# Halved weight units, squares moved behind the splits, and first loads on two queues in a streaming encoder step

## The chip, the cores and the metric

The kernel runs on one core of a Trainium2 chip. The metric is device time in microseconds (us), from runs without a profiler: the median of three runs of the kernel before is 1717.9 us (1715.5 to 1718.19). The engines are named PE (TensorE), DVE (VectorE), ACT (ScalarE), POOL (GpSimd) and SP (SyncE). Each works through its own list of instructions in order and meets the others only at semaphores.

## The reference, cut to what matters

One step of a two-layer encoder for 2048 prompt frames and 64 sample frames, 1024 features each, in float32. Layer A is a recurrent block, layer B attention over a short window.

```python
def _layer_a(x, ...):
    u = _rmsnorm(x, norm_g) @ w_in            # 1024 -> 2048
    xb, gate = jnp.split(u, 2, axis=-1)
    xc, new_buf = _causal_conv(xb, conv_buf, cw, cb)
    h, h_last = _rglru(xc, h0, ...)
    y = (h * silu(gate)) @ w_out
    return x + y, ...
# then k, v from one projection, and layer B: norm, projection to queries
# and gate, attention, output projection, residual
```

The change works on the first projection, `_rmsnorm(x, norm_g) @ w_in`, and on how all weights are prepared. The norm's factor of a frame is taken behind the matmul: the sum of squares over the features is made beside it, and the projection's result is multiplied by one over the root.

## The kernel before, in words

**Precision.** Every float32 matmul is made of three: a value is split into a high part (a copy in the matmul's rounded format, made by ACT) and a low part (the value less its high part), and high times high, low times high and high times low are summed. This holds for inputs and weights.

**Weights.** There are 54 units of 128 x 1024: unit u is one block of 128 output columns of a projection. Of these, 0 to 15 are the first projection's, 16 to 19 the gates', 20 and 21 the keys' and values', 22 to 29 the first output projection's, 30 to 45 the second projection's, 46 to 53 the last one's. A unit is loaded into `raw`, a buffer for two units (`load_unit`, a DMA issued by POOL); ACT makes the high part (`high_part`), and for units 0 to 3 DVE, for the others POOL, makes the low part (`low_part`); `low_units` is POOL's loop: low part of unit u, then the load of unit u+2, which waits until the low part of unit u is done. `VECTOR_UNITS` (4) is the number of units whose low part DVE makes. `w_high` and `w_split` count the finished parts, and PE waits for `w_split` before it uses a unit.

**The first projection.** The 2112 frames are worked in 6 tiles of 352. In step s the inputs of tile s are split while PE multiplies tile s-1. For each of a tile's 8 blocks of 128 features ACT makes the high part and then the square (`high_input`), DVE makes the low part and then adds the square to a running sum `acc` (`low_input`). There is one buffer `m.sq` for the square, so the square of block n waits until that of block n-1 has been added. Step 0 only splits: blocks 0 to 7, and behind blocks 0, 2, 4 and 6 the weight units 0 to 3, unit 4 behind block 7. In step 1, place j (0 to 15) PE multiplies unit j, ACT makes the high part of unit 5+j, and of input block j-3 of the next tile. After unit 0 PE sums `acc` over the features with a matmul by ones (L591), ACT takes the root (L410), DVE the reciprocal (L496). Only then does DVE start on the results: for j below 8 `branch` multiplies by the factor (L527) and makes the convolution (L531 to L561), for j from 8 it multiplies only (L514) and ACT applies SiLU (L433). PE has four result banks: unit j waits until result j-4 has been read.

**Later stages that the weights touch.** The last step of the projection (s = 6) splits units 16 to 26, the recurrent stage units 27 to 29 in turns of its own and 30 to 38 at its end, the second projection 39 to 45 and 46 to 53. In the recurrent stage POOL also makes parts of the scan's operands (L1031, L1039, L1042, L1050), in order with its weight work.

**Start of the program.** SP issues the loads of `vec`, `sink` and `halo` and then the 8 input blocks of tile 0; POOL issues units 0 and 1. ACT and DVE wait for all three small loads (`const_loaded`) before their first work on them.

## Time and profile before

| | |
|---|---|
| median of 3 runs | 1717.9 us |
| profiled execution, first to last instruction (span) | 1712.8 us |
| what lies around the span, by the median | 5.1 us |
| PE busy | 1612.5 us, 94% |
| PE weight load busy | 1457.1 us, 85% |
| DVE busy | 1182.5 us, 69% |
| ACT busy | 709.7 us, 41% |
| POOL busy | 393.2 us, 23% |

The profiled execution gives only its span, so its time as a run is taken to be the median. In the profile a row of the timeline is an instruction (or several merged, x2): start, duration, engine, line, operation, output and input, and in brackets how long the engine had been idle and what ended the wait. A group row gives the count, the busy time with the mean in ns, and the idle time ahead of the group.

### The profile page before, as it was taken

What the parts mean: (1) busy time and instruction counts of PE and PEld (TensorE: products, weight loads), DVE (VectorE), ACT (ScalarE), POOL (GpSimd) and SP (SyncE); (2) the same over time, 40 slices, a digit from 0 to 9 for tenths busy, and PEclk for the clock granted to TensorE, in tenths of its full rate; (3) what the DMA queues carried; (4) which work ended last, traced back from release to release, by engine and by line L of the source; (5) the groups of instructions that cost most, each with busy time, mean ns of one, the idle gap of its engine ahead of it and who ended that gap; (6) DMA issues with size and microseconds to landing.
All of it is one profiled execution on the core that took longest, in us unless ns stands there. A gap on an engine that the chain in (4) does not pass through costs nothing.

```text
span 1712.8 us, 30967 instructions
## 1 busy us (share of the span) xinstructions
PE 1612.5 (94%) x10611; PEld 1457.1 (85%) x10611; DVE 1182.5 (69%) x2355; ACT 709.7 (41%) x1560; POOL 393.2 (23%) x304
## 2 busy tenths in 40 slices
PE   6899999998699999997889999999899999999999
PEld 5799999998689999997889999999846777777778
DVE  7964674585699999998667476484587666666661
ACT  4322212225866777752343343343443333333330
POOL 4400000044665555554320000003111111111110
PEclk8999999999799999999999999999999999999999
DMA  5431221243333333325431121124323322332212
GB/s 171 130 113 55 82 75 59 73 144 105 92 111 109 103 103 109 101 79 167 107 123 60 51 90 52 62 80 131 106 64 96 106 72 64 104 100 75 62 38 74
DMA packets 160802, 158.25 MB, mean 92 GB/s; under 512 B 53681, under 2 KB 153777, under 8 KB 160689
## 3 DMA queue, kind: packets, MB, share of 16 engines
q1 hardware_dynamic: 142544, 119.86, 23.4%
q0 software_dynamic: 7776, 28.32, 5.4%
q10 hardware_dynamic: 10368, 8.66, 1.5%
q8 instruction: 61, 1.00, 0.2%
q14 instruction: 53, 0.43, 0.1%
HBM read 102.68 MB, written 54.36 MB: 92 GB/s over the span
## 4 chain that ended last, share of the span: by engine, by line
PE 53%; DVE 13%; issue 5%; ACT 3%; DMA 2%; SPq 1%; POOL 0%; DVEq 0%; ACTq 0%; POOLq 0%
PE s_banks L585 18%; PE bank L1374 11%; PE bank L1359 4%; PE bank L1361 4%; PE bank L1118 3%; DVE r_th L859 3%; PE s_banks L1315 3%; PE s_banks L1087 2%; DVE r_x_hi L883 2%; PE bank L1330 2%; PE bank L1332 2%; DMA b_x<-x_dram 1%; PE bank L570 1%; DVE r_x L879 1%; PE bank L585 1%
## 5 line engine op out<-in xcount | busy, mean ns | idle before, releaser
L629 POOL TENSOR_TENSOR w_lo_a<-w_raw,w_hi_a 128x1024 fp32r<-128x1024 f32 x28 | 67.0, 2391 | 616.2 <-ACT w_hi_a L624 616.1
L1544 ACT ACTIVATE m_p<-s_banks,m_nm 128x192 f32<-128x192 f32 (+2 forms) x264 | 106.3, 415 | 235.4 <-DVE m_nm L1425 235.4
L1374 PE MATMUL bank<-m_y_hi,w_hi_a 128*128 128x256 f32 (+1 forms) x512 | 149.0, 291 | 0.6 <-DVE m_out L1475 0.6
L1374 PE MATMUL bank<-m_y_lo,w_hi_a 128*128 128x256 f32 (+1 forms) x512 | 144.0, 281 | 0.0
L1374 PE MATMUL bank<-m_y_hi,w_lo_a 128*128 128x256 f32 (+1 forms) x512 | 143.8, 281 | 0.0
L585 PE MATMUL bank<-a_hi,w_hi_a 128*128 128x352 f32 x384 | 127.7, 332 | 15.9 <-DVE w_lo_a L629 11.3
L1588 POOL TENSOR_TENSOR m_y_lo<-m_y,m_y_hi 128x256 fp32r<-128x256 f32 x66 | 48.6, 737 | 399.5 <-DVE m_y_hi L1467 399.5
L585 PE MATMUL s_banks<-b_hi,w_hi_a 128*128 128x352 f32 x384 | 129.9, 338 | 0.0
L585 PE MATMUL bank<-a_hi,w_lo_a 128*128 128x352 f32 x384 | 125.7, 327 | 0.0
L585 PE MATMUL bank<-a_lo,w_hi_a 128*128 128x352 f32 x384 | 125.6, 327 | 0.0
L585 PE MATMUL s_banks<-b_hi,w_lo_a 128*128 128x352 f32 x384 | 123.9, 323 | 0.0
L585 PE MATMUL s_banks<-b_lo,w_hi_a 128*128 128x352 f32 x384 | 123.9, 323 | 0.0
L475 DVE RECIPROCAL b_qstd<-b_qstd 128x352 f32<-128x352 f32 x48 | 112.6, 2346 | 8.4 <-ACT b_qstd L429 5.5
L1118 PE MATMUL bank<-r_y_hi,w_hi_b 128*128 128x264 f32 x384 | 110.5, 288 | 2.7 <-ACT r_std L1008 2.7
L551 DVE SCALAR_TENSOR_TENSOR a_out<-a_xb,vec,a_out 128x352 f32<-128x352 f32 (+2 forms) x168 | 108.4, 657 | 5.1
L1118 PE MATMUL bank<-r_y_lo,w_hi_b 128*128 128x264 f32 x384 | 110.5, 288 | 0.0
L1118 PE MATMUL bank<-r_y_hi,w_lo_b 128*128 128x264 f32 x384 | 110.0, 286 | 0.0
L585 PE MATMUL bank<-a_hi,w_hi_b 128*128 128x352 f32 x288 | 94.3, 328 | 9.7 <-DVE a_xb L527 6.0
L585 PE MATMUL s_banks<-b_hi,w_hi_b 128*128 128x352 f32 x288 | 101.8, 353 | 0.0
L1374 PEld LDWEIGHTS bank<-m_y_hi,w_hi_a 128*128 128x128 f32 x512 | 96.3, 188 | 1.2 <-issue 1.2
L1374 PEld LDWEIGHTS bank<-m_y_lo,w_hi_a 128*128 128x128 f32 x512 | 96.6, 189 | 0.0
L1374 PEld LDWEIGHTS bank<-m_y_hi,w_lo_a 128*128 128x128 f32 x512 | 96.3, 188 | 0.0
(196 smaller groups left out, 4978.7 us busy)
## 6 DMA issues: line engine op xcount, KB each, us to landing
w_raw<-weights_dram POOLq DMA_DIRECT2D x54, 512.0 KB, 4.0
a_x<-xT_dram SPq DMA_DIRECT2D x48, 176.0 KB, 2.3
xc_dram<-a_out SPq DMA_DIRECT2D x48, 176.0 KB, 1.8
sga_dram<-a_out SPq DMA_DIRECT2D x48, 176.0 KB, 1.8
r_xc<-xc_dram SPq DMA_DIRECT2D x32, 264.0 KB, 3.0
r_sg<-sga_dram SPq DMA_DIRECT2D x32, 264.0 KB, 2.7
r_x<-xT_dram SPq DMA_DIRECT2D x64, 132.0 KB, 2.2
x_dram<-r_x SPq DMA_DIRECT2D x64, 132.0 KB, 1.8
```

The source lines that it names most:

```text
L475: nc.vector.reciprocal(m.qstd[:, :], m.qstd[:, :]).then_inc(m.qrec_done, 1)
L551: op = nc.vector.scalar_tensor_tensor(out=out, in0=x, scalar=vec[:, CW + tap, j:j + 1], in1=out, op0=ALU.mult, op1=ALU.add)
L585: mm = nc.tensor.matmul(m.banks[j % 4][:, 0:PT], w[pw][:, kt * P:(kt + 1) * P], x[:, kt, :], start=(n == 0), stop=(n == 3 * NB - 1))
L629: ops.tensor_tensor(low, raw[:, u % 2, :], high.bitcast(F32), ALU.subtract).then_inc(w_split, 1)
L859: i = nc.vector.tensor_tensor_scan(r.th[:, q, blk, :], r.a[:, q, blk, :], r.ti[:, q, blk, :], h_last[:, c:c + 1], ALU.mult, ALU.add)
L1118: mm = nc.tensor.matmul(bank[4 + blk % 2][:, 0:RT], w[pw][:, kt * P:(kt + 1) * P], (r.y_hi, r.y_lo)[px][tp][:, kt, :], start=(i == 0), sto ...
L1315: mm = nc.tensor.matmul(s_banks[:, 2 * (i % 2) + e, bp * 192 + v0:(bp + 1) * 192], m.q[par][rows, j, blk:blk + 2, :].rearrange("p b t -> p ...
L1359: nc.tensor.matmul(out, m.v[par][:, j, n * HEAD:(n + 1) * HEAD], m.pt_a[:, e * AT:(e + 1) * AT], start=True, stop=False, skip_group_check= ...
L1361: mm = nc.tensor.matmul(out, m.v[par][HEAD:P, j + 1, n * HEAD:(n + 1) * HEAD], m.pt_b[HEAD:P, e * AT:(e + 1) * AT], start=False, stop=True ...
L1374: mm = nc.tensor.matmul(out_bank(ts, blk)[:, 0:width], w[pw][:, kt * P:(kt + 1) * P], (m.y_hi, m.y_lo)[px][tp][:, kt, 0:width], start=(n = ...
L1544: nc.scalar.activation(m.p[:, q, k, v0:192], s_banks[:, 2 * q + e, bp * 192 + v0:(bp + 1) * 192], ACT.Exp, bias=m.nm[:, q, k:k + 1], accum ...
L1588: nc.gpsimd.tensor_tensor(y_part(m.y_lo, s, par, i), m.y[:, q, :, :], y_part(m.y_hi, s, par, i).bitcast(F32), ALU.subtract).then_inc(m.y_l ...
```

## The change

Four things are changed together. (1) `raw` becomes four half buffers; each unit is loaded, split high and split low in halves of 128 x 512, each with its own semaphore step, and the load of a half of unit u+2 waits only for the low part of that half of unit u. In step 1 PE waits for each half of a unit by itself. (2) In step 0 ACT makes the high parts of all 8 input blocks first, with units 0, 1 and 2 behind blocks 0, 3 and 6, and then the 8 squares, with unit 3 behind square 2 and unit 4 behind square 5; DVE makes all low parts, then all additions. The first projection's `m.sq` has two buffers. (3) DVE makes the low parts of units 0 and 1 only, POOL from unit 2 on. (4) Input blocks 1, 3, 5 and 7 of tile 0, `sink` and `halo` are issued by ACT; ACT and DVE wait at first for `vec` alone.

```diff
-        raw = sb("w_raw", [P, 2, D])
+        raw = sb("w_raw", [P, 4, HALF])
-                m.sq, m.acc = b(f"{tag}_sq", [P, 1, PT]), b(f"{tag}_acc", [P, 1, PT])
+                m.sq, m.acc = b(f"{tag}_sq", [P, 2, PT]), b(f"{tag}_acc", [P, 1, PT])
+        def square_input(eng, m, s, blk):
+            nx, nq, n = m.x.shape[1], m.sq.shape[1], NB * s + blk
+            need(eng, m.sq_added, n + 1 - nq)
+            nc.scalar.activation(m.sq[:, blk % nq, :], m.x[:, blk % nx, :], ACT.Square).then_inc(m.sq_done, 1)
...
+            if m.first_weights:
+                for blk in range(NB):
+                    high_input(eng, m, 0, 0, blk)
+                    if blk % 3 == 0:
+                        high_part(eng, m.unit + blk // 3)
+                for blk in range(NB):
+                    square_input(eng, m, 0, blk)
+                    if blk in (2, 5):
+                        high_part(eng, m.unit + 2 + (blk + 1) // 3)
...
+            if m.first_weights:
+                for blk in range(NB):
+                    low_input(eng, m, 0, 0, blk)
+                    if blk == 0 or blk == 3:
+                        low_part(eng, nc.vector, m.unit + blk // 3)
+                for blk in range(NB):
+                    add_input(eng, m, 0, blk)
...
+                        if isinstance(s, int) and s == 1 and n % (3 * NB // 2) == 0:
+                            split(eng, m.unit + j, kt // (NB // 2))
...
-        VECTOR_UNITS = 4
+        VECTOR_UNITS = 2
+        def load_half(eng, u, half):
+            if u >= 2:
+                split(eng, u - 2, half)
+            k = 2 * (u % 2) + half
+            eng.dma_start(raw[:, k, :], A["weights"][u, :, half * HALF:(half + 1) * HALF]).then_inc(raw_loaded[k], 16)
...
         def low_units(eng, first, end):
             for u in range(first, end):
-                if u >= VECTOR_UNITS:
-                    low_part(eng, nc.gpsimd, u)
-                if u + 2 < UNITS:
-                    load_unit(eng, u + 2)
+                for half in range(2):
+                    if u >= VECTOR_UNITS:
+                        low_half(eng, nc.gpsimd, u, half)
+                    if u + 2 < UNITS:
+                        load_half(eng, u + 2, half)
...
         @block.scalar
-            eng.wait_ge(const_loaded, 16 * N_CONST)
+            for blk in range(1, NB, 2):
+                load_input(eng, a1, 0, blk)
+            eng.dma_start(sink[:, :], A["sinks"]).then_inc(const_loaded, 16)
+            eng.dma_start(halo[:, :, :], conv0).then_inc(const_loaded, 16)
+            eng.wait_ge(vec_loaded, 16)
```

`high_part` and `low_part` become loops over the two halves; all other waits of PE on a unit wait for its second half.

## Rows read from the trace of the kernel before

**Rows 1.** Busy time by stretch: us, PE, PEld, DVE, ACT, POOL, clock, DMA, GB/s
```profile
5.00:8.00 3.00, 0.00 (x0) 0.00 (x0) 0.31 (x3) 0.57 (x3) 0.00 (x0) 1.00 1.06 360
22.60:28.30 5.70, 5.70 (x17) 5.20 (x18) 3.00 (x4) 3.76 (x4) 4.40 (x4) 0.50 0.39 118
57.80:83.00 25.20, 17.85 (x97) 16.80 (x97) 22.75 (x49) 10.99 (x17) 12.38 (x7) 0.93 0.44 140
83.00:350.00 267.00, 266.98 (x1652) 265.62 (x1653) 152.49 (x335) 65.54 (x120) 6.55 (x5) 1.00 0.24 78
```

**Rows 2.** What PE waited for in the first 100 us: us, times, longest
```profile
PE bank L585 <- DVE w_lo_a L629: 11.3, 1, 11.3
PE bank L585 <- DVE a_xb L527: 4.1, 3, 2.6
PE bank L585 <- POOL w_lo_b L629: 1.2, 1, 1.2
```

**Rows 3.** Timeline of the start: loads issued, first work of ACT
```profile
1.29 1.23 POOL L604 DMA_DIRECT2D w_raw<-weights_dram  x2 [0.82 <-POOLq L1722]
2.15 7.27 SPq L339 DMA_DIRECT2D a_x<-xT_dram  x9
7.85 0.59 ACT L348 ACTIVATE a_hi<-a_x,vec 128x352 fp32r<-128x352 f32 x1 [1.41 <-DMA a_x<-xT_dram]
8.35 0.48 ACT L351 ACTIVATE a_sq<-a_x 128x352 f32<-128x352 f32 x1
8.73 1.04 ACT L624 ACTIVATE w_hi_a<-w_raw 128x1024 fp32r<-128x1024 f32 x1
```

**Rows 4.** DMA issues by line: count, KB each, median us to landing
```profile
a_x<-xT_dram SPq DMA_DIRECT2D x9, 176.0 KB, 5.4
...
w_raw<-weights_dram POOLq DMA_DIRECT2D x54, 512.0 KB, 4.0
```

**Rows 5.** Timeline around the sum of squares: last addition to first result
```profile
22.45 0.52 DVE L366 TENSOR_TENSOR a_acc<-a_acc,a_sq 128x352 f32<-128x352 f32 x1
...
23.63 1.38 PE L591 MATMUL s_banks<-a_acc,ones 128*128 128x352 f32 x2
...
25.63 2.35 DVE L496 RECIPROCAL a_std<-a_std 128x352 f32<-128x352 f32 x1 [2.67 <-ACT a_std L410]
...
28.02 0.59 DVE L527 TENSOR_TENSOR a_xb<-bank,a_std 128x64 f32<-128x64 f32 x2
```

**Rows 6.** Groups of POOL by shape: count, busy us, mean ns
```profile
L629 POOL TENSOR_TENSOR w_lo_a<-w_raw,w_hi_a 128x1024 fp32r<-128x1024 f32 x28 | 67.0, 2391 | 616.2 <-ACT w_hi_a L624 616.1
...
L1588 POOL TENSOR_TENSOR m_y_lo<-m_y,m_y_hi 128x256 fp32r<-128x256 f32 x66 | 48.6, 737 | 399.5 <-DVE m_y_hi L1467 399.5
```

**Rows 7.** Timeline of DVE and POOL: convolution steps without and beside POOL
```profile
47.41 2.22 DVE L551 SCALAR_TENSOR_TENSOR a_out<-a_xb,vec,a_out 128x64 f32<-128x64 f32 x6
...
51.83 4.27 DVE L551 SCALAR_TENSOR_TENSOR a_out<-a_xb,vec,a_out 128x64 f32<-128x64 f32 x6
...
52.08 2.76 POOL L629 TENSOR_TENSOR w_lo_b<-w_raw,w_hi_b 128x1024 fp32r<-128x1024 f32 x1 [9.47 <-ACT w_hi_b L624]
55.14 0.58 POOL L604 DMA_DIRECT2D w_raw<-weights_dram  x1 [0.30 <-POOL w_lo_b L629]
...
77.05 0.52 DVE L514 TENSOR_TENSOR a_out<-bank,a_std 128x352 f32<-128x352 f32 x1
```

**Rows 8.** Timeline of ACT: squares that waited, and the first SiLU
```profile
50.55 0.50 ACT L351 ACTIVATE a_sq<-a_x 128x352 f32<-128x352 f32 x1 [10.83 <-DVE a_acc L363]
...
77.17 0.50 ACT L351 ACTIVATE a_sq<-a_x 128x352 f32<-128x352 f32 x1 [4.73 <-DVE a_acc L366]
...
78.97 0.50 ACT L433 ACTIVATE a_out<-a_out 128x352 f32<-128x352 f32 x1
```

**Rows 9.** Timeline of the recurrent stage: a weight unit beside the scan
```profile
472.40 2.79 POOL L629 TENSOR_TENSOR w_lo_b<-w_raw,w_hi_b 128x1024 fp32r<-128x1024 f32 x1 [1.50 <-ACT w_hi_b L624]
...
472.81 5.20 DVE L859 TENSOR_TENSOR_SCAN r_th<-r_a,h_last,r_ti 128x264 f32<-128x264 f32 x2
```

More of the change, by code:

```diff
@@ L43 @@
 NG = 4
+HALF = D // 2
 SLOTS_A, SLOTS_B, SLOTS_C = 8, 6, 2
@@ L365, in low_input @@
                 eng.wait_ge(m.sq_added, n)
-                nc.vector.tensor_tensor(m.acc[:, 0, :], m.acc[:, 0, :], m.sq[:, 0, :], ALU.add)\
+                nc.vector.tensor_tensor(m.acc[:, 0, :], m.acc[:, 0, :], m.sq[:, blk % nq, :], ALU.add)\
                   .then_inc(m.sq_added, 1)
         def run_project(eng, m, body):
-            if m.first_weights:
+            if m.first_weights and eng is not nc.scalar and eng is not nc.vector:
                 body(0, 0)
@@ L384, in body @@
                         starts[j]()
-                    if known(s, 0, PN - 1) and j < NB:
+                    if known(s, 0, PN - 1) and j < NB and not (isinstance(s, int) and s == 0 and j % 2):
                         load_input(eng, m, s, j)
@@ L486, in continue_input @@
                     low_input(eng, m, s, par, blk)
-                unit = project_unit(m, s, j)
-                if unit and unit[0] < VECTOR_UNITS:
-                    low_part(eng, nc.vector, unit[0])
+                    add_input(eng, m, s, blk)
                 after(s, j)
@@ L577, in body @@
                 for j in range(2 * NB):
-                    eng.wait_ge(w_split, m.unit + j + 1)
                     need(eng, m.evacuated, 2 * NB * t + j - 3)
@@ L597, in project_tensor, with split @@
             run_project(eng, m, body)
-        VECTOR_UNITS = 4
-        def load_unit(eng, u):
-            need(eng, w_split, u - 1)
-            eng.dma_start(raw[:, u % 2, :], A["weights"][u, :, :]).then_inc(raw_loaded[u % 2], 16)
+        VECTOR_UNITS = 2
+        def split(eng, u, half=1):
+            if u < VECTOR_UNITS:
+                eng.wait_ge(w_split_first, 2 * u + half + 1)
+            else:
+                eng.wait_ge(w_split, 2 * (u - VECTOR_UNITS) + half + 1)
+        def load_half(eng, u, half):
[3 more added lines that the diff above has]
+            eng.dma_start(raw[:, k, :], A["weights"][u, :, half * HALF:(half + 1) * HALF]).then_inc(raw_loaded[k], 16)
         SLOTS_IN_B = (list(range(UNITS_GATE)) + list(range(UNITS_GATE + UNITS_KV, SLOTS_A + SLOTS_B))
@@ L619, in high_part, with low_half @@
         def high_part(eng, u, freed=None, count=0):
-            eng.wait_ge(raw_loaded[u % 2], 16 * (u // 2 + 1))
             if freed is not None:
                 eng.wait_ge(freed, count)
-            nc.scalar.activation(slot_of(u)[0], raw[:, u % 2, :], ACT.Copy).then_inc(w_high, 1)
+            for half in range(2):
+                k = 2 * (u % 2) + half
+                eng.wait_ge(raw_loaded[k], 16 * (u // 2 + 1))
+                nc.scalar.activation(slot_of(u)[0][:, half * HALF:(half + 1) * HALF], raw[:, k, :], ACT.Copy)\
+                  .then_inc(w_high, 1)
         def low_part(eng, ops, u):
+            for half in range(2):
+                low_half(eng, ops, u, half)
+        def low_half(eng, ops, u, half):
             high, low = slot_of(u)
-            eng.wait_ge(w_high, u + 1)
-            ops.tensor_tensor(low, raw[:, u % 2, :], high.bitcast(F32), ALU.subtract).then_inc(w_split, 1)
+            at = slice(half * HALF, (half + 1) * HALF)
+            eng.wait_ge(w_high, 2 * u + half + 1)
+            ops.tensor_tensor(low[:, at], raw[:, 2 * (u % 2) + half, :], high[:, at].bitcast(F32), ALU.subtract)\
+               .then_inc(w_split_first if u < VECTOR_UNITS else w_split, 1)
         def low_units(eng, first, end):
             for u in range(first, end):
-                if u >= VECTOR_UNITS:
-                    low_part(eng, nc.gpsimd, u)
-                if u + 2 < UNITS:
-                    load_unit(eng, u + 2)
+                for half in range(2):
+                    if u >= VECTOR_UNITS:
+                        low_half(eng, nc.gpsimd, u, half)
+                    if u + 2 < UNITS:
+                        load_half(eng, u + 2, half)
         def place(j):
@@ L655, in project_unit @@
                 return None
-            if m.first_weights and s == 0 and j in (0, 2, 4, 6, 8):
-                return (m.unit + j // 2,)
             if m.first_weights and s == 1 and j + 5 < 2 * NB:
@@ L1598, in _ @@
             nc.disable_value_cache = True
-            eng.dma_start(vec[:, :, :], A["vec"]).then_inc(const_loaded, 16)
-            eng.dma_start(sink[:, :], A["sinks"]).then_inc(const_loaded, 16)
-            eng.dma_start(halo[:, :, :], conv0).then_inc(const_loaded, 16)
+            eng.dma_start(vec[:, :, :], A["vec"]).then_inc(vec_loaded, 16)
             recurrent_sync(eng)
@@ L1614, in _ @@
         def _(eng):
-            load_unit(eng, 0)
-            load_unit(eng, 1)
+            for u in range(2):
+                for half in range(2):
+                    load_half(eng, u, half)
             nc.gpsimd.memset(ident[:, :], 0.0).then_inc(const_pool, 1)
@@ L1645, in _ @@
                   .then_inc(const_made, 1)
-            eng.wait_ge(const_loaded, 16 * N_CONST)
-            nc.vector.tensor_scalar(neg_sink[:, :], sink[:, :], -1.0, None, ALU.mult).then_inc(const_made, 1)
+            eng.wait_ge(vec_loaded, 16)
             nc.vector.tensor_scalar(kq_scale[:, :], vec[:, QN, 0:1], HEAD ** -0.5, None, ALU.mult)\
```

25 lines of the change are left out of this document (16 added, 9 removed).

## The prediction, made before the changed kernel was run

> **What bounds the kernel now.** I read the busy time by stretch first. From 83 to 350 us PE is busy 266.98 of 267.00 us [rows 1]: a microsecond won ahead of 83 us comes out at 350 us unchanged. From 57.8 to 83 us PE works 17.85 of 25.20 us while DVE works 22.75: here DVE sets the pace. The waits of PE say where: 11.3 us at the start until DVE has the low part of unit 0, then 4.1 us in three waits for DVE's reading of results (L527), and last 1.2 us for POOL's low part of unit 13 [rows 2]. So the start has three pieces in series: (a) up to DVE's reciprocal at 25.63 [rows 5]; (b) DVE's eight branches, from 28.02 [rows 5] to the first L514 at 77.05 [rows 7], 49.0 us, through which DVE has no gap; (c) unit 12 and the wait for unit 13. PE's long first wait is in none of them: when PE starts unit 0 matters only through the reciprocal, and units 1 to 4 run at a granted clock of 0.50 (of 2.4 GHz, so 1.2) and still are not what DVE waits for [rows 1].
>
> **(a) Up to the reciprocal.** Before, ACT starts on block 0 at 7.85, when that block lands; it was issued at 2.15 behind three small loads [rows 3], and these loads took 5.4 us [rows 4] while the DMA engines moved 360 GB/s [rows 1]. After, SP issues it behind `vec` only: three issues take 0.76 to 2.15, so about 1.2. Half of the blocks no longer stand ahead of the others on one queue, and the two units arrive in halves between them. Bytes are the same (1.4 MB of input, 1.0 MB of weights, 7 us at 360 GB/s), so the last of them lands near 9.7, but block 0 near 4.9. ACT is ready at about 5.2: it must first issue six DMAs (0.35 to 0.45 us each, by SP's spacing), load its table, and do two small operations. That is 2.6 us earlier than before.
>
> ACT's work from there: start to start a high input takes 0.50 (7.85 to 8.35), a square 0.38 (8.35 to 8.73), a unit 0.95 [rows 3]; a half unit, by the slope between 352 and 1024 columns (0.67 ns each), 0.61, so a unit in halves 1.22, 0.27 more. I followed the order: block 0, unit 0 (its second half lands at 6.7) to 7.3, blocks 1 to 3 to 8.8, unit 1 (second half 9.8) to 10.4, blocks 4 to 6 to 11.9, unit 2 to 13.1, block 7 to 13.6, squares 0 to 2 to 14.8, unit 3 to 16.0, squares 3 to 5 to 17.3. Then unit 4. Its halves are loaded only when POOL has finished the low halves of unit 2, which were DVE's units before. A low half on POOL costs 1.29 us (between 0.737 for 256 columns and 2.391 for 1024 [rows 6]), its load issue 0.30 + 0.58 [rows 7]: 2.17 us per half, 4.3 per unit against 2.39 + 0.88 = 3.3 before. POOL takes unit 2 from 12.6 to 13.9 and from 14.7 to 16.0; a half lands some 3.2 us after its issue (4.0 for a unit [rows 4] less 0.7 for 256 KB at 360 GB/s), so unit 4's second half is there at 19.4. ACT finishes it at 20.0, squares 6 and 7 at 20.8, and DVE the last addition at 21.3, against 22.97 before [rows 5]. PE has been through unit 0 since about 15 (block 7's low part is there at 14.1) and takes the sum at once, where it was 0.66 us late before (22.97 to 23.63). The sum's 1.38, the root and their handovers put the reciprocal at 23.6: **-2.0 us**. From both sides: if nothing holds ACT, its 5.2 + 8 x 0.50 + 5 x 1.22 + 8 x 0.38 = 18.3 gives a reciprocal at 20.5, -5.1; if the input comes little earlier or the chain through unit 4 slips by 2 us, 0. I take the worked chain, nearer to the lower end.
>
> **(b) DVE's eight branches.** Six steps of the convolution take 2.22 us alone and 4.27 beside a POOL low part of 2.76 [rows 7]: DVE loses 2.05 us to each such unit. Between 28.02 and 77.05 there are seven (units 6 to 12) and 0.9 us of unit 5: 15.4 of the 49.0, so 33.6 are DVE's own. After, unit 5 falls wholly into the stretch: eight units. The cost of one in halves: POOL holds DVE for 2 x 1.29 = 2.58 instead of 2.39, and each time some 0.35 of it (2.39 less 2.05) hides under work that DVE has in flight: 1.9; where the second hiding doesn't come, 2.2; if each half also costs a handover, 2.5. At 2.0 the stretch takes 33.6 + 16.0 = 49.6: **+0.5**. Bounds: 1.7 each (-1.8) and 2.5 each (+4.6). Two buffers for squares let ACT run one block ahead (it sat 10.83 us at 50.55 on the single buffer, and 4.73 at each later block [rows 8]); this moves POOL's units to earlier places of the same stretch, not out of it, and is worth nothing here.
>
> **(c) Unit 13.** The square of block 5 waited until 77.17, then ACT loaded a table, and SiLU came at 78.97 [rows 8], the high part of unit 13 behind it. With the second buffer that square is long done and the table loaded when the first L514 ends; the high part starts 1.4 us earlier (77.57, where L514 ends, to 78.97), and PE needs only a half. The 1.2 us go [rows 2]: **-1.2**. Then PE is late by nothing: by POOL's 4.3 us a unit the first half of unit 14 is done about 1.1 us before PE asks for it, that of unit 15 0.6. If POOL fails to keep up with PE's 3.88 (24 matmuls of 267/1652 = 0.162 [rows 1]), the term is 0.
>
> **Later stages.** Units 27 to 29 stand in POOL's list ahead of the operands of the scan, and DVE's two scans take 5.20 us because they stand behind such a unit's 2.79 us [rows 9]. Two halves and two issues cost POOL 1.0 us more, ACT 0.3; part of it falls into POOL's waiting for DVE. I take +0.5 for each of the three. At the end of the recurrent stage nine units (30 to 38) meet short DVE operations; a half blocks for 1.3 instead of 2.4 and DVE gets its turn between: -1.0 in all. In the last step of the first projection seven units (16 to 22) meet the branches as in (b); POOL then waits long for DVE, so its slower pace is covered: 0. Sum **+0.5**, bounds -1.5 and +5.0 (three times 1.0, and two for the rest). The moved `neg_sink` (0.17) and the `halo` load are needed after 23 us: 0. In tiles 2 to 5 only the order of ACT and DVE operations changes, under a full PE: 0.
>
> **Sum.** -2.0 + 0.5 - 1.2 + 0.5 = -2.2 us. The profiled span of 1712.8 would be 1710.6; with the 5.1 around it, 1717.9 becomes **1715.7 us**. A difference under 0.2% (3.4 us) is about what a measurement of this kernel can't tell from none.
>
> **Rivals.**
> *Free start (faster).* Unit 4 arrives in time, and ACT's row of work is the only limit of (a): -5.1 + 0.5 - 1.2 + 0.5 = -5.3, 1712.6. For it: ACT's own work ends at 18.3. Against it: unit 4 hangs on two POOL halves and a load of over 3 us. Chance 0.28.
>
> *POOL's price (slower).* Every unit costs POOL 4.3 us instead of 3.3 and locks DVE twice. If a unit in halves costs DVE 2.5 us, (b) grows by 4.6, and if POOL's extra microsecond lands on the scan in full at units 27 to 29, 3.0 more come: -2.0 - 1.2 + 4.6 + 3.0 = +4.4, 1722.3. It decides from a cost of 2.3 us a unit on. For it: DVE has no cover in (b), and POOL is in the loop of the scan. Against: the lock follows POOL's reading time, which grows by 0.2 only. Chance 0.18.
>
> *The wires are full (no change).* Inputs don't come as early as I say because the DMA engines are the limit at 360 GB/s [rows 1]; only the 0.95 us of earlier issue is kept. ACT starts at 6.9, and 1.7 of the 2.0 in (a) are lost: -0.5, 1717.4. For it: the 5.4 us to landing [rows 4] are bandwidth. Against: block 0 alone needs 176 KB, and the order of arrival changes. Chance 0.12. The Trainium skill, DMA: Bandwidth & Descriptors, section "Issuing engines are not separate DMA queues", speaks for this one: loads started from several engines share the same 16 DMA engines, and starting them concurrently saves only the time the sequencer needs to issue them. By that rule the second queue itself brings under a microsecond; the trace so far agrees in that the bytes in flight from 5 to 8 us already fill the engines.
>
> **How the numbers follow.** The forecast has 0.42, its own range 1713.8 to 1717.6; a quarter of it lies beyond 0.2% faster. Faster: 0.28 + 0.10 = 0.38. Same: 0.32 + 0.10 (full wires) = 0.42. Slower: 0.18 + 0.02 = 0.20. The range takes in the free start with a good (b) and most of the slower case: 1709.5 to 1721.5.
>
> **What would show it.** (a) ACT's first high input near 5.2, unit 4's second high half near 19.5, the reciprocal near 23.6. If the first is near 7, the wires are full. (b) First L514 49.6 + 2.4 us behind the reciprocal's start; each POOL half beside DVE costs it about 1.0. (c) No PE wait for POOL near 80. Later: turns with units 27 to 29 longer by half a microsecond. The prediction is wrong if (b) grows by over 2 us, or if the gain at 350 us is not in the end.

## The result: slower by 0.9%, and the profile after

The changed kernel takes **1733.3 us** (median; 1731.8 to 1734.7), beside 1716.9 us of the kernel before on the same chip: a ratio of 1.0093, 95% interval 1.0080 to 1.0107. The forecast of 1715.7 us was wrong, and 1733.3 lies outside its range; the side on which it fell is that of the rival "POOL's price", at over three times that rival's size (16.3 us by the medians for its 4.4). The profiled execution has a span of 1732.8 us (time 1734.7) against 1712.8. Between span and time of one execution lie 1.7 to 2.2 us in all runs here; so the profiled execution of before took some 1714.7 us, about 2 below its median (the 5.1 us given above as lying around its span are mostly that), and the 20.0 us between the two spans are more than the 16.3 between the medians.

The waits of PE in the first 100 us of the kernel after (us, times, longest), which answer to [rows 2]:

```profile
PE s_banks L620 <- DVE a_acc L377: 10.2, 1, 10.2
PE bank L614 <- DVE w_lo_a L675: 9.9, 1, 9.9
PE bank L614 <- DVE a_xb L546: 9.6, 4, 3.7
```

The wait for POOL is gone, as forecast, and the first wait is 1.4 us shorter. But a new one of 10.2 us stands first: the matmul of the sum of squares waits for DVE's additions, where before it waited for nothing but its turn. And the waits for DVE's reading of results have more than doubled, from 4.1 to 9.6 us. Both point at DVE. Its timeline after (start, us, engine, line, operation, tiles, count, idle time before), from the additions to the second branch, answers to [rows 5, 7]:

```profile
15.88 0.96 DVE L364 SCALAR_TENSOR_TENSOR a_lo<-a_x,vec,a_hi 128x352 fp32r<-128x352 f32 x1 [0.57 <-ACT a_hi L351]
16.76 0.33 DVE L374 COPY a_acc<-a_sq 128x352 f32<-128x352 f32 x1
17.20 7.38 DVE L377 TENSOR_TENSOR a_acc<-a_acc,a_sq 128x352 f32<-128x352 f32 x5
25.30 2.96 DVE L377 TENSOR_TENSOR a_acc<-a_acc,a_sq 128x352 f32<-128x352 f32 x2 [0.73 <-ACT a_sq L358]
...
30.48 2.35 DVE L515 RECIPROCAL a_std<-a_std 128x352 f32<-128x352 f32 x1 [2.14 <-ACT a_std L421]
32.87 0.59 DVE L546 TENSOR_TENSOR a_xb<-bank,a_std 128x64 f32<-128x64 f32 x2
33.37 1.18 DVE L550 COPY a_xb<-halo 128x3 f32<-128x3 f32 x1
...
36.90 6.87 DVE L570 SCALAR_TENSOR_TENSOR a_out<-a_xb,vec,a_out 128x64 f32<-128x64 f32 x6
43.69 1.77 DVE L576 COPY halo_sample<-a_xb 128x3 f32<-128x3 f32 x1
```

Five additions that take 0.52 us each in [rows 5] take 7.38; six convolution steps that took 2.22 alone and 4.27 beside POOL [rows 7] take 6.87; a copy of three columns takes 1.77. What POOL does in these microseconds:

```profile
16.75 0.56 POOL L642 DMA_DIRECT2D w_raw<-weights_dram  x1 [0.30 <-POOL w_lo_a L675]
17.33 1.29 POOL L675 TENSOR_TENSOR w_lo_a<-w_raw,w_hi_a 128x512 fp32r<-128x512 f32 x1
18.92 0.56 POOL L642 DMA_DIRECT2D w_raw<-weights_dram  x1 [0.30 <-POOL w_lo_a L675]
19.50 1.27 POOL L675 TENSOR_TENSOR w_lo_a<-w_raw,w_hi_a 128x512 fp32r<-128x512 f32 x1
...
36.99 0.56 POOL L642 DMA_DIRECT2D w_raw<-weights_dram  x1 [0.30 <-POOL w_lo_a L675]
37.57 1.31 POOL L675 TENSOR_TENSOR w_lo_a<-w_raw,w_hi_a 128x512 fp32r<-128x512 f32 x1
39.17 0.56 POOL L642 DMA_DIRECT2D w_raw<-weights_dram  x1 [0.30 <-POOL w_lo_a L675]
39.75 1.31 POOL L675 TENSOR_TENSOR w_lo_a<-w_raw,w_hi_a 128x512 fp32r<-128x512 f32 x1
```

The durations of POOL are the forecast ones (1.29, 0.30 and 0.56 for 0.58). Its pattern is not the one of before: POOL runs turn behind turn (a turn is the issue of a load and the low part behind it), 2.17 us each, and DVE gets one or two operations per turn: the second and third addition take 2.05 us each, two others, which fell where POOL waited for ACT, 0.52. The forecast let DVE work in the 0.87 us between two low parts.

The same is seen most cleanly in the last tile, where a convolution is three steps. First a row of the kernel before, then the same line after:

```profile
353.16 3.90 DVE L551 SCALAR_TENSOR_TENSOR a_out<-a_xb,vec,a_out 128x352 f32<-128x352 f32 x3
```
```profile
361.82 6.37 DVE L570 SCALAR_TENSOR_TENSOR a_out<-a_xb,vec,a_out 128x352 f32<-128x352 f32 x3
370.55 6.35 DVE L570 SCALAR_TENSOR_TENSOR a_out<-a_xb,vec,a_out 128x352 f32<-128x352 f32 x3
...
387.90 1.83 DVE L570 SCALAR_TENSOR_TENSOR a_out<-a_xb,vec,a_out 128x352 f32<-128x352 f32 x3
```

Alone three steps take 1.83 us; after, 6.37, which is 2.12 a step: POOL's turn of 2.17, once per step.

**Where the 20.0 us of span arose.** I took the start of the same operation in every kernel's trace and subtracted that of before: DVE's first reciprocal (25.6 us before), its first result of a gate block (77.0), the second reciprocal (101.5), the end of the last tile (391.0, the reciprocal on `lw`), the scan behind unit 29 (498.6), the first maximum of the attention (1232.3), the last one (1663.5). Differences in us, of one profiled execution each. The ratio is that of the measured times, with its 95% interval, against the runs of before that go with the kernel (their medians lie between 1715.7 and 1717.3); it is not simply the quotient of two medians. In the names, whole and halves are the units' size, dve4 and dve13 the number of units whose low parts DVE makes; each run is told below.

| kernel | recip. 1 | gate | recip. 2 | last tile | scan | attention | its end | median us | ratio |
|---|---|---|---|---|---|---|---|---|---|
| after | +4.8 | +9.8 | +8.0 | +12.4 | +13.7 | +11.8 | +20.0 | 1733.3 | 1.0093 [1.0080, 1.0107] |
| e1_halves | -2.7 | +2.5 | +1.9 | +6.3 | +7.6 | +3.7 | +9.3 | 1726.1 | 1.0050 [1.0035, 1.0066] |
| e2_whole | +4.9 | +4.2 | +2.5 | +1.6 | +1.7 | -0.9 | +7.3 | 1725.0 | 1.0046 [1.0031, 1.0062] |
| e3_dve4 | +0.9 | +5.6 | +3.7 | +8.1 | +9.4 | +6.3 | +9.4 | 1726.3 | 1.0058 [1.0037, 1.0079] |
| e4_act_issue | +1.2 | +0.2 | -1.8 | +2.6 | +3.9 | -0.3 | +7.6 | 1723.3 | 1.0028 [1.0011, 1.0044] |
| e11_after_dve | +4.0 | -1.1 | -2.9 | +1.5 | +2.9 | -1.3 | +4.4 | 1720.8 | 1.0027 [1.0014, 1.0041] |
| e5_before_dve13 | +0.2 | -5.6 | -6.7 | -7.6 | -7.6 | -9.0 | -5.6 | 1706.9 | 0.9926 [0.9903, 0.9949] |
| e6_halves_dve13 | -1.9 | -7.4 | -9.1 | -4.6 | -3.3 | -6.8 | -5.2 | 1713.6 | 0.9975 [0.9960, 0.9989] |
| e7_both_tiles | -3.0 | -8.5 | -10.2 | -12.4 | -12.9 | -12.8 | -0.6 | 1709.2 | 0.9939 [0.9919, 0.9959] |
| e8_whole_both | -0.1 | -5.9 | -7.0 | -9.1 | -12.0 | -13.7 | -14.7 | 1699.9 | 0.9913 [0.9892, 0.9933] |
| e9_whole_both_sq2 | -1.4 | -7.2 | -8.7 | -10.8 | -13.6 | -14.9 | -12.1 | 1700.8 | 0.9904 [0.9882, 0.9925] |
| e10_start_alone | +2.2 | +2.4 | +2.2 | +1.4 | +1.3 | -1.4 | +6.7 | 1722.6 | 1.0034 [1.0020, 1.0048] |
| e12_start_alone2 | -0.6 | -0.7 | -1.0 | -1.8 | -1.7 | -4.6 | +4.6 | 1718.3 | 1.0013 [1.0001, 1.0025] |
| e13_all | -2.0 | -7.8 | -9.5 | -11.6 | -14.5 | -17.0 | -4.9 | 1705.0 | 0.9923 [0.9899, 0.9947] |

For the kernel after, 11.8 us stand when the attention begins and 8.2 more come inside it, where all these kernels do the same work (the last low part of a weight lies ahead of it in every trace). Busy time by stretch, before and then after (us; PE, PEld, DVE, ACT, POOL busy; granted clock; DMA share; GB/s):

```profile
1220.00:1280.00 60.00, 52.28 (x298) 33.73 (x298) 39.44 (x121) 26.27 (x104) 10.09 (x10) 0.91 0.29 83
...
1480.00:1540.00 60.00, 58.92 (x404) 41.80 (x401) 37.89 (x111) 20.92 (x86) 5.90 (x8) 1.00 0.30 85
```
```profile
1220.00:1280.00 60.00, 52.98 (x283) 38.87 (x282) 33.04 (x88) 25.45 (x79) 7.97 (x8) 0.83 0.37 100
...
1480.00:1540.00 60.00, 57.66 (x381) 41.25 (x379) 35.32 (x103) 19.32 (x80) 5.16 (x7) 0.94 0.28 78
```

The granted clock was 0.91 and 1.00 in these stretches before, 0.83 and 0.94 after: more time at 1.2 GHz. The stretches are the same times, not the same work, since the attention begins 11.8 us later after; from its first maximum on, the first 40 us had a granted clock of 0.87 before and 0.74 after. All fifteen traces say the same. From the first maximum to the last the attention takes 430.1 to 443.3 us, in the order of the time in it at a granted clock of 0.50:

| us at 0.50 | kernels | us of attention |
|---|---|---|
| 10.2 | before, e6, e8 | 430.1 to 432.7 |
| 13.7 | e3 | 434.2 |
| 20.5 | e1, e5, e9, e11 | 434.0 to 436.9 |
| 27.3 | after, e2, e4, e10 | 439.1 to 439.4 |
| 30.7 | e12 | 440.4 |
| 37.5 | e7, e13 | 443.2 to 443.3 |

By a straight line through the fifteen, a microsecond at the lower clock costs 0.44. So compare kernels by the column "attention"; the last three also hold this, and it can differ between executions of one kernel (the mean clock of a whole run was 0.979 to 0.986 in the four of e5).

### The profile page after: what moved, and what is told of

It is laid out like the page before. It is cut to its first block, busy times and chain, and to the rows that moved or that the text cites. A ratio compares the mean times of both kernels' runs of the same rounds, so it can differ in the third digit from the quotient of the medians.

```text
span 1732.8 us, 31085 instructions
## 1 busy us (share of the span) xinstructions
PE 1619.9 (93%) x10611; PEld 1462.4 (84%) x10611; DVE 1203.0 (69%) x2355; ACT 715.7 (41%) x1614; POOL 435.5 (25%) x412
## 4 chain that ended last, share of the span: by engine, by line
PE 51%; DVE 15%; issue 5%; ACT 2%; DMA 2%; SPq 0%; POOL 0%; DVEq 0%; ACTq 0%; POOLq 0%
PE s_banks L614 18%; PE bank L1422 11%; PE bank L1407 4%; PE bank L1409 4%; DVE r_th L905 3%; PE s_banks L1363 3%; DVE r_x_hi L929 3%; PE bank L1378 2%; PE bank L1166 2%; PE bank L1380 2%; PE s_banks L1135 2%; PE bank L598 1%; DVE r_x L925 1%; DVE r_th L881 1%; PE bank L614 1%
## 5 line engine op out<-in xcount | busy, mean ns | idle before, releaser
L675 POOL TENSOR_TENSOR w_lo_a<-w_raw,w_hi_a 128x512 fp32r<-128x512 f32 x60 | 77.7, 1297 | 595.6 <-ACT w_hi_a L664 594.7
L614 PE MATMUL bank<-a_hi,w_hi_a 128*128 128x352 f32 x384 | 129.1, 336 | 20.5 <-DVE w_lo_a L675 9.9
L570 DVE SCALAR_TENSOR_TENSOR a_out<-a_xb,vec,a_out 128x352 f32<-128x352 f32 (+2 forms) x168 | 115.2, 697 | 5.1
```

The lines of the kernel that those rows point to most:

```text
L570: op = nc.vector.scalar_tensor_tensor(out=out, in0=x, scalar=vec[:, CW + tap, j:j + 1], in1=out, op0=ALU.mult, op1=ALU.add)
L614: mm = nc.tensor.matmul(m.banks[j % 4][:, 0:PT], w[pw][:, kt * P:(kt + 1) * P], x[:, kt, :], start=(n == 0), stop=(n == 3 * NB - 1))
L675: ops.tensor_tensor(low[:, at], raw[:, 2 * (u % 2) + half, :], high[:, at].bitcast(F32), ALU.subtract)\
```

## The experiments

**Theory 1.** A DVE operation with two SBUF inputs that starts just as POOL issues a transfer with a low part ready right behind is held until that low part has ended; back-to-back turns of POOL leave DVE about one such operation each. **Rivals:** the low halves themselves cost DVE (by number or by POOL's time), or the late arrival of the first weights does it.

**m1_port** measures this alone, in one execution, and computes nothing of the reference: 24 DVE steps of 128x64 with two SBUF inputs, beside a list of POOL work, in eight phases.

```python
        #   name: POOL's list; a = low part, d = load, w = wait for ACT
        phases = ["", "aaaa", "dddd", "dadadada", "dwadwadwadwa", "AA", "dAdA", "adadadad"]
```

> Leaves out all of the reference: eight phases, in each 24 DVE steps of 64 columns with two SBUF inputs (scalar_tensor_tensor) beside a list of POOL work; a is a low part of 512 columns, A of 1024, d the issue of a 256 KB load, w a wait of about 1 us for ACT. Phases: nothing; aaaa; dddd; dadadada; dwadwadwadwa; AA; dAdA; adadadad. Theory 1 (the issue and the low part right behind it hold DVE as one piece: a DVE step that starts during the issue ends only with the low part): nothing about 5 us for 24 steps; dddd about the same; in dadadada the longest steps take 1.8 to 2.1 us and only one or two steps fit between two low parts, where the gap of 0.87 us has room for four; with w between issue and low part (dwa) the longest steps fall to about 1.4 and several steps run during each issue. Theory 2 (DVE is held only while POOL reads, 1.3 us, with a fixed loss at each handover): the longest steps take 1.3 to 1.6 us in dadadada and in dwa alike, and about four steps fit into each gap of both.

DVE's timeline, one row per phase in the order of the list:

```profile
5.30 4.79 DVE L158 SCALAR_TENSOR_TENSOR t_out<-t_x,t_s,t_y 128x64 f32<-128x64 f32 x24 [3.21 <-ACTq L171]
10.26 8.90 DVE L158 SCALAR_TENSOR_TENSOR t_out<-t_x,t_s,t_y 128x64 f32<-128x64 f32 x24 [0.17 <-ACTq L171]
19.33 4.79 DVE L158 SCALAR_TENSOR_TENSOR t_out<-t_x,t_s,t_y 128x64 f32<-128x64 f32 x24 [0.17 <-ACTq L171]
25.38 10.60 DVE L158 SCALAR_TENSOR_TENSOR t_out<-t_x,t_s,t_y 128x64 f32<-128x64 f32 x24 [1.27 <-ACTq L171]
36.16 8.11 DVE L158 SCALAR_TENSOR_TENSOR t_out<-t_x,t_s,t_y 128x64 f32<-128x64 f32 x24 [0.17 <-ACTq L171]
46.37 9.02 DVE L158 SCALAR_TENSOR_TENSOR t_out<-t_x,t_s,t_y 128x64 f32<-128x64 f32 x24 [2.10 <-ACTq L171]
55.55 10.18 DVE L158 SCALAR_TENSOR_TENSOR t_out<-t_x,t_s,t_y 128x64 f32<-128x64 f32 x24 [0.17 <-ACTq L171]
65.91 10.45 DVE L158 SCALAR_TENSOR_TENSOR t_out<-t_x,t_s,t_y 128x64 f32<-128x64 f32 x24 [0.17 <-ACTq L171]
```

Nothing beside it: 4.79 us. Four issues alone (third row): 4.79, an issue costs DVE nothing. Four low parts alone: +4.11, 1.03 each, in four steps of 1.30 to 1.32. Issue and low part directly behind one another (fourth row): +5.81, 1.45 each. With a pause between issue and low part (fifth row) the excess is 3.32, but only three low parts met DVE's steps: 1.11 each, in steps of 1.38. So the join costs 0.3 to 0.4 us a turn more. It comes from a few very long steps, one of the fourth row and one of the seventh (low parts of 1024 columns):

```profile
25.98 3.90 DVE L158 SCALAR_TENSOR_TENSOR t_out<-t_x,t_s,t_y 128x64 f32<-128x64 f32 x1
26.34 1.27 POOL L109 TENSOR_TENSOR w_lo<-w_raw,w_hi 128x512 f32<-128x512 f32 x1
27.54 0.56 POOL L112 DMA_DIRECT2D w_land<-weights_dram  x1
28.12 1.27 POOL L109 TENSOR_TENSOR w_lo<-w_raw,w_hi 128x512 f32<-128x512 f32 x1
...
55.95 5.67 DVE L158 SCALAR_TENSOR_TENSOR t_out<-t_x,t_s,t_y 128x64 f32<-128x64 f32 x1
```

The first step starts at 25.98, while an issue is under way (25.79 to 26.32), and is held over two whole low parts, though an issue alone holds nobody. That is longer than the 1.8 to 2.1 us that had been expected. It does not happen at every join: at the last one of the fourth row three steps of 0.27 us ran during the issue (31.10 to 31.65 us), the third across the start of the low part. So the sequence issue, low part often acts as one piece, and two turns can merge; what decides when it does, these runs don't show.

**e4_act_issue** takes this into the kernel: ScalarE issues the loads of units 2 to 16, POOL makes the same low halves.

```diff
...
             for half in range(2):
+                if 1 <= u <= 15:
+                    load_half(eng, u + 1, half)
                 k = 2 * (u % 2) + half
...
-                    if u + 2 < UNITS:
+                    if 17 <= u + 2 < UNITS:
```

> The kernel after, but the raw weight halves of units 2 to 16 are loaded by ScalarE's queue (issued just ahead of the high part of the unit before) instead of POOL's; POOL makes the same low halves in the same order, with no transfer issue between them. Theory 1 (a VectorE step with two SBUF inputs that starts as POOL begins a transfer issue with a low part right behind it is held through both, and that is what made the additions and the first tile's branches long): the additions L377 of tile 0 fall from 2.05 us each to below 1.0, the first branch from 12.6 to about 8 us, the eight branches of tile 0 from 53.9 to about 49.5, and the whole to about 1727. Rival (POOL's low parts themselves take the time, whoever issues the transfers): nothing moves, 1732 to 1735. ScalarE's waits ahead of its issues may cost up to 2 us in either case.

The additions and the first two convolutions in its timeline:

```profile
16.77 1.16 DVE L378 TENSOR_TENSOR a_acc<-a_acc,a_sq 128x352 f32<-128x352 f32 x2
18.65 5.95 DVE L378 TENSOR_TENSOR a_acc<-a_acc,a_sq 128x352 f32<-128x352 f32 x5 [0.72 <-ACT a_sq L359]
...
32.62 6.19 DVE L571 SCALAR_TENSOR_TENSOR a_out<-a_xb,vec,a_out 128x64 f32<-128x64 f32 x6
...
40.27 2.21 DVE L571 SCALAR_TENSOR_TENSOR a_out<-a_xb,vec,a_out 128x64 f32<-128x64 f32 x6
```

The eight branches take 48.0 us (29.20 to 77.21) instead of 53.9, and the first reciprocal comes 3.7 us earlier than in the kernel after. At the attention all of the 11.8 us lost are back (-0.3), with as many low halves on POOL: the number of halves was not the cause, the issue in front of them was. Per half that is 0.37 us in the branches ((53.9 - 48.0) / 16), the size of the join in m1_port. The transfers were no faster (behind the first four, the median half landed 3.0 us after its issue from either engine); that they may have started earlier is not parted from this. The measured time, 1723.3, is better than expected but still above before: its profiled run goes from -0.3 to +7.6 within the attention. The first branch, expected at 8 us, took 9.7: six low halves ran back to back (7.62 us) beside it and cost DVE 3.98 in six steps, so low parts alone hold DVE as well, only less. Nor did the additions fall below 1.0 us each as expected: three of the seven took 1.40 or 1.41 (2.05 in the kernel after).

**e11_after_dve** removes POOL from the branches in another way: DVE makes the low parts of units 5 to 12.

```diff
+                unit = project_unit(m, s, j)
+                if unit and 5 <= unit[0] <= 12:
+                    if unit[0] == 5:
+                        split(eng, 4)
+                    low_part(eng, nc.vector, unit[0])
...
-                    if u >= VECTOR_UNITS:
+                    if u >= VECTOR_UNITS and not 5 <= u <= 12:
```

> The kernel after with VectorE making the low parts of units 5 to 12 (beside the branches of tile 0); everything up to the first reciprocal stays as in the kernel after. Theory 1: the first reciprocal stays 4.9 us later than before, the branches of tile 0 fall from 53.9 to 43.5 us, so the eighth branch ends about 0.5 us earlier than before instead of 9.9 later, the second reciprocal about 2 us earlier, the last tile's halves on POOL add 4.4 us: about 1719 to 1722. Rival (the branches are long because PE or the weights are late after the late reciprocal): they stay above 50 us, 1730.

The branches take 43.9 us (31.98 to 75.90), the first reciprocal stays 4.0 late, and 1720.8 was measured: near theory 1 on every point.

**e1_halves** (halves alone; order, start and square buffer as before), **e2_whole** (the change with whole units) and **e3_dve4** (the change, but DVE makes the low parts of units 0 to 3 as before) part the change.

```diff
# e2_whole
-HALF = D // 2
+PARTS = 1
+HALF = D // PARTS
...
# e3_dve4
-                    if blk == 0 or blk == 3:
+                    if blk % 3 == 0:
                         low_part(eng, nc.vector, m.unit + blk // 3)
...
+                    if blk == 2:
+                        low_part(eng, nc.vector, m.unit + 3)
...
-        VECTOR_UNITS = 2
+        VECTOR_UNITS = 4
```

> The kernel before with the halves alone (units loaded and split in halves through four half buffers; step 0, DVE's units 0 to 3 and the start of the program as before, one buffer for squares). If the halves are the cause through POOL's turns (theory 1, and theory 2 alike), everything from the first branch on is as in the changed kernel: branches of tile 0 +4 to +5 us, those of the last tile +4, units 27 to 29 +1, so 1726 to 1729. If the cause lay in the new order or the start of step 0, this kernel is within 2 us of the kernel before.

> The changed kernel with whole units again (two buffers of 1024 columns, one load, one high and one low part each); the new order of step 0, DVE's share of two units, two square buffers and the loads on two queues are kept. Theory 1: branches of both tiles as before (0), the wait for unit 13 gone (-1.5), but in step 0 POOL's issue plus low part (0.56 + 2.4 us) now hold DVE's additions, one per POOL turn of 3.3 us, so the reciprocal comes at 27 to 31 instead of 25.6: 1717 to 1721. If only halves hurt, the reciprocal is at 24 and the time 1713 to 1715.

> The changed kernel with the low parts of units 2 and 3 back on DVE (behind input block 6 and behind the third addition), so that POOL works beside DVE's additions for unit 4 only. Theory 1: the additions are no longer held, the reciprocal comes at 23.5 to 26 instead of 30.5, the rest stays as in the changed kernel: 1727 to 1729. If step 0 is slow for another reason (loads that land late, ACT's order), the reciprocal stays near 30 and the time at 1733.

Read in the table: e1 has its first reciprocal 2.7 us early and then loses 5.2 in the branches (gate minus reciprocal) and 4.4 in the last tile. e2 has the late reciprocal in full (+4.9) and loses nothing in the branches (gate minus reciprocal -0.7) nor in the last tile (-0.9). So halves cost in both tiles of branches, and the late reciprocal is no matter of halves: it comes of POOL's units 2 and 3 standing beside the additions. e3 confirms that: with these two on DVE it shrinks from 4.8 to 0.9. The 0.9 is still 3.6 later than in e1, which has the old order and the old start; how much of that is the order and how much the start in halves, no run parts. In time e1 met its expectation; e2 (1725.0) missed its 1717 to 1721 through the attention (from -0.9 to +7.3), and e3 (1726.3) came out just under its 1727, with the reciprocal at 26.5 for 23.5 to 26.

**e5_before_dve13** asks the opposite question of the kernel before: what is POOL's whole share of tile 0 worth?

```diff
-        VECTOR_UNITS = 4
+        VECTOR_UNITS = 13
```

> The kernel before with VectorE making the low parts of units 0 to 12 (before: 0 to 3), so POOL makes none beside the branches of tile 0 but only issues their transfers. Theory 1: a branch of tile 0 loses what POOL's turn cost it (about 2.0 us a unit by the stretches of before) and takes on one low part of 1.22 us on VectorE: eight branches 49.0 to about 43, and the whole to about 1711 to 1713. Rival (VectorE is only given more work, since what it waits for in these branches is not POOL): 8 x 1.22 more, about 1722 to 1726.

```profile
28.23 0.59 DVE L527 TENSOR_TENSOR a_xb<-bank,a_std 128x64 f32<-128x64 f32 x2
28.73 0.16 DVE L531 COPY a_xb<-halo 128x3 f32<-128x3 f32 x1
...
29.64 2.22 DVE L551 SCALAR_TENSOR_TENSOR a_out<-a_xb,vec,a_out 128x64 f32<-128x64 f32 x6
...
31.92 1.22 DVE L629 TENSOR_TENSOR w_lo_a<-w_raw,w_hi_a 128x1024 fp32r<-128x1024 f32 x1
33.05 0.58 DVE L527 TENSOR_TENSOR a_xb<-bank,a_std 128x64 f32<-128x64 f32 x2
```

The convolution is at its 2.22 us, DVE's own low part costs 1.22, and eight branches take 43.2 instead of 49.0. Less its eight low parts of 1.22 that leaves 33.4 us for DVE's own work, where the forecast had worked out 33.6. 1706.9 us, ratio 0.9926: one changed number makes the kernel faster than either, and better than expected. The rival (more work on the pacing engine) is out: beside branches DVE pays 2.05 us for a low part that POOL makes and 1.22 for one of its own.

**e6_halves_dve13** and **e7_both_tiles** put this on halves: e6 is e1 with `DVE_UNITS = range(13)`; e7 adds units 16 to 22, beside the last tile's branches, and the second square buffer. **e8_whole_both** is e5 with units 16 to 22 and **e9_whole_both_sq2** adds the buffer.

```diff
-        VECTOR_UNITS = 4
+        DVE_UNITS = (*range(13), *range(16, 23))
...
-                if u >= VECTOR_UNITS:
+                if u not in DVE_UNITS:
```

> Units in halves with the order, the start and the single square buffer of before (as e1_halves) and VectorE makes the low parts of units 0 to 12. e1_halves had its first reciprocal 2.6 us early and its eight branches 5.2 us longer than before. Theory 1: the early reciprocal is kept and the branches take about 43.5 us, so tile 0 ends about 8 us earlier than in the kernel before; the last tile still has POOL's halves (+4.4 us beside its branches): about 1712. Rival (halves cost by their number, on whatever engine): the branches stay at 52 to 54 us, about 1726.

> As e6_halves_dve13, and VectorE makes the low parts of units 16 to 22 too (beside the last tile's branches), and two square buffers. Theory 1: the last tile's branches lose the 4.4 us that POOL's halves had added and some 3 to 5 us that whole units already cost in the kernel before, and the reciprocals of tiles 1 and on come about 1.5 us earlier: about 1704. Rival (VectorE paces the last tile's branches by its own work): 7 x 1.22 us more there, about 1716 to 1720.

> The kernel before with VectorE making the low parts of units 0 to 12 and 16 to 22, so POOL makes none beside either tile of branches that shares its time with weights. e5_before_dve13 (0 to 12 alone) had tile 0 end 5.8 us early and measured 1706.9. Theory 1: the last tile's branches, where the kernel before still has POOL's issue and low part of seven whole units, lose 3 to 5 us more: about 1703. Rival (in the last tile VectorE's own work is the pace, and POOL's low parts were hidden): 7 x 1.22 us more there, minus nothing, about 1712 to 1715. The gain of a stage can be eaten by a longer stretch at the lower clock at the next transition, as in e7_both_tiles.

> As e8_whole_both with two square buffers (the change's own part that gave back 1.7 us at the second reciprocal): about 1.5 us less than e8 at that reciprocal, so about 1701 to 1702. Rival: in whole units the second reciprocal waits for unit 13 to 15 and not for the squares, nothing moves, 1703.

e6 came out at 1713.6, near its 1712; e8 3 us better than its 1703. The last tile of e8, whose convolutions took 3.90 us in the kernel before:

```profile
345.69 1.82 DVE L553 SCALAR_TENSOR_TENSOR a_out<-a_xb,vec,a_out 128x352 f32<-128x352 f32 x3
348.63 1.83 DVE L553 SCALAR_TENSOR_TENSOR a_out<-a_xb,vec,a_out 128x352 f32<-128x352 f32 x3
```

By the last tile's end this brings only 1.5 us over e5, since DVE now has seven low parts of its own; just behind it, where the gates need units 16 to 19, it grows to 4.4 us (scan) and stays (4.7 at the attention); why there I have not traced. **e8 is the fastest kernel of the study, 1699.9 us, with e9 level (1700.8; the intervals of the ratios overlap for the most part).** e9 is 1.7 us ahead of e8 at the second reciprocal, where 1.5 were expected; 1.3 of it is there at the first one already, so the second buffer works mostly in step 0. At the attention 1.2 are left; the measurement doesn't show them. e7 missed its 1704 by 5 us: near e8 until the attention (-12.8 to -13.7), it lost 12 us in it, with 37.5 us at the lower clock for 10.2.

**e10_start_alone** and **e12_start_alone2** are the kernel before with the change's first loads alone (part 4). In e10 I had put DVE's wait for `sink` and `halo` ahead of its first low part; e12 has it behind the last addition.

> The kernel before with the change's first loads alone (odd input blocks, sink and halo on ScalarE's queue, vec by itself ahead; whole units, order and square buffer of before). In the kernel after the inputs landed within 3.5 us of their issue but the first weight half only after 7.0 us, against 4.3 us before. Theory A (three queues share what the first transfers can have, the weights pay for the inputs): the first whole unit lands 2 to 4 us later than before, the first reciprocal comes 0 to 3 us later, 1717 to 1720. Rival B (the late weight halves came of being four transfers instead of two, not of the third queue): the first reciprocal comes 1 us earlier, about 1716.

> As e10_start_alone, but VectorE's wait for sink and halo stands behind the last addition of tile 0 and no longer ahead of its first low part. In e10 that wait ended at 11.2 us and the low part of block 0, possible at 6.0, started at 11.28, so the run could not tell what the three queues do. There the first whole unit's high part began at 7.93 us, 0.8 us earlier than in the kernel before. Theory A (in whole units the start on three queues passes 0.8 us on): the first reciprocal 0.8 us earlier than before, and the whole 1 us below the kernel before. Rival B (the first units land too late for the order of before, with block 1 or unit 1 late behind them): the first reciprocal level with before or up to 1 us later, the whole 0 to 2 us above.

> e9_whole_both_sq2 with this start. By theory A its first reciprocal comes 0.8 us earlier than in e9 (there 1.4 us earlier than before), and the whole is 1700, less the 0.8: 1699 to 1700. Rival: what the start gives is lost at the next change of stage by the clock, 1700 to 1702; a difference of 1 us lies within the interval of the ratio, so the reciprocals decide.

e10's low part of block 0 started at 11.28 us behind that wait; the run says nothing on its question. e12 does: ACT's first high part at 5.49 (before 7.85), and then the wait for the weights.

```profile
5.49 0.57 ACT L351 ACTIVATE a_hi<-a_x,vec 128x352 fp32r<-128x352 f32 x1
5.97 0.48 ACT L358 ACTIVATE a_sq<-a_x 128x352 f32<-128x352 f32 x1
8.13 1.06 ACT L649 ACTIVATE w_hi_a<-w_raw 128x1024 fp32r<-128x1024 f32 x1 [1.68 <-DMA w_raw<-weights_dram]
```

The 2.4 us by which the input comes earlier become 0.6 at the first unit (8.13 for 8.73 [rows 3]) and 0.6 at the reciprocal. At the attention 4.6 us are gained, 2.8 of them behind the scan, which I have not traced further. The measured time is no better than before (1.0013, 1.0001 to 1.0025), and e13, e9 with this start, is 4 us above e9 (the intervals of the ratios, 0.9923 and 0.9904, overlap) and above the 1699 to 1702 expected, in spite of being 2.1 ahead at the attention. In the same stretch as above, e12:

```profile
1220.00:1280.00 60.00, 52.84 (x251) 31.35 (x249) 35.49 (x111) 23.97 (x96) 9.86 (x9) 0.74 0.30 76
```

0.74 where before had 0.91: fewer matmuls (x251 against x298) in the same 60 us, though the attention began 4.6 us earlier. That the lower clock takes the gain is shown by the rows and by the table of the attention; what makes it fall longer in one kernel than in another is not, and was not tried by itself.

## Why the prediction was wrong

**The step that failed is the cost of a unit in halves, 2.0 us, in (b), with the same assumption in (a).** I took POOL's 0.87 us of handover and issue as a gap for DVE. In the traces it was one when POOL then waited for data. Before, seven whole units fell into the 49.0 us, POOL waited for each one's high part, and low parts began by themselves ([rows 7] shows 9.47 us of idle time before one; I read the 2.05 us off just such a one). In halves the next high part is there when POOL asks, issue and low part join, and DVE is often held through both. The cost was 2.54 us a unit on the average of the branches ((53.9 - 33.6) / 8), above the 2.3 from which the slower rival was to decide; e4 put the join away and came to (48.0 - 33.6) / 8 = 1.8.

A second step failed besides: the attention, in which nothing changes, was put at nothing, and in the profiled runs it is the largest single term, through the clock. Without it the 11.8 us at its start would still have been beyond the range, whose upper end lay 3.6 us above before.

Term by term, as the table gives them (forecast, measured, in us):

- (a) to the reciprocal: -2.0, **+4.8**. ACT was in time on block 0 (5.75, forecast 5.2). The first weight halves were not: 8.30 and 9.78, forecast 6.7 for the second. I had shared the engines' 360 GB/s evenly; on three queues the first three input blocks (landed by 4.9) went ahead of the weights (8.28). Block 7's high part started 2.2 us late (15.27 for 13.1). Then POOL's units 2 and 3 ran beside the additions: end 28.3 for 21.3. I had followed ACT, POOL and the loads through this stretch, and given DVE its undisturbed 0.52 us per addition.
- (b) eight branches: +0.5, **+4.9**, above the upper bound of +4.6.
- (c) unit 13: -1.2, **-1.7**. Right: the wait of PE for POOL is gone from the list.
- later: +0.5, **+3.8** (last tile +4.4, units 27 to 29 +1.3, from the scan to the attention -1.9). "POOL then waits long for DVE, so its slower pace is covered" failed in the last tile: POOL's pace was covered, DVE's was not. The other two were +1.3 for a forecast of +1.5 and -1.9 for -1.0.
- the attention: 0, **+8.2** in the profiled runs. Not in the forecast at all. The medians are 16.3 us apart, so if the 11.8 hold in every run, some 4.5 is its usual size.

The rival "POOL's price" had the right engine and, for (b), the size: 2.54 us a unit for its 2.5, +4.9 for its +4.6. It kept (a) at -2.0, though, gave nothing to the last tile, and had no term for the attention; and its reason, a handover for each half, was not the one that the runs showed. "The wires are full" was wrong for the input (ACT 5.75) and right for the weights. Of the rule it leaned on (the Trainium skill, DMA: Bandwidth & Descriptors, "Issuing engines are not separate DMA queues"), e12's trace agrees with its sum: 0.6 us gained at the reciprocal from the second queue and the shorter wait together.

What would have warned me stands late in the trace of before, where DVE has two-input operations beside two units in a row. DVE, then POOL:

```profile
771.04 2.96 DVE L901 TENSOR_TENSOR r_acc<-r_acc,r_sq 128x264 f32<-128x264 f32 x1
...
770.72 0.60 POOL L604 DMA_DIRECT2D w_raw<-weights_dram  x1 [0.30 <-POOL w_lo_a L629]
771.34 2.36 POOL L629 TENSOR_TENSOR w_lo_a<-w_raw,w_hi_a 128x1024 fp32r<-128x1024 f32 x1
```

An addition of 264 columns starts at 771.04, inside the issue and 0.30 us ahead of the low part, and ends at 774.00, 0.30 behind it. The low part came second and DVE waited all the same. I had looked for the price only in the branches.

## What to carry to other kernels

When POOL shares a stage with a pacing DVE, ask not only how long POOL's operation is but whether it starts alone or directly behind a DMA issue: moving the issue to another engine, or the work to DVE itself (1.22 us for 2.05 to 2.5), was worth more here than the change's other parts (e4 10 us below the kernel after, e8 17 below before; the start alone, e12, nothing that the times show). Cutting work in halves filled the pauses in which another engine had lived. And compare stages by their landmarks as well as by the whole time: from 1232 us on, the clock blurred differences of up to 12 us.

## What the runs showed of the hardware

- An issue of a transfer by POOL holds no DVE operation by itself (4.79 us for 24 steps with or without four of them), but with a low part directly behind it the pair often acts as one hold: single steps of 3.90 us (over two low parts of 512 columns) and 5.67 (two of 1024); at one of the joins three steps ran free. Per low part DVE lost 1.45 us joined, 1.03 without issues. The Trainium skill, SBUF — State Buffer, "SBUF: two separate sides", has DVE and GpSimd take turns on a shared pair of ports, each for one whole instruction. The phase with low parts alone agrees (steps of 1.30 us for low parts of 1.26); the joined turns are longer than that rule gives.
- A copy of 128x3, 0.16 us alone, took up to 1.77 beside joined turns in the kernel after: it is not only operations with two inputs that are held.
- With loads on three queues the first four weight halves (256 KB each) of the kernel after landed 7.0 to 8.8 us after their issue, the first three input blocks (176 KB) 2.8 to 3.7 us after theirs, the others 7.7 to 9.8. On two queues the first two whole units (512 KB) had taken 4.3 and 5.4. The first half varies, though: with the same first loads it took 4.3 us in e4 and 6.1 in e3.
- In the first 40 us of the attention the granted clock was 0.87 before, 0.74 after and 0.62 in e12, for the same work, though from 1160 to 1220 us PE was busy 60.00 of 60.00 us at a clock of 1.00 in each of the three. Over fifteen traces a microsecond at 0.50 in the attention went, by a straight line, with 0.44 us of time.
